# Probabilities and values split into parts and multiplied over 512 queries in three attention stages

## What is computed

```python
# neighbourhood: each query sees a clamped 8 x 16 window of the grid
s = einsum('bhrcd,bhrikd->bhrcik', qg, kg) * d ** -0.5 + bias
s = where(valid[:, None, :], s, NEG)
pr = softmax(s.reshape(B, H, R, GRID_W, kr * GRID_W), axis=-1)
o = einsum('bhrcik,bhrikd->bhrcd', pr, vg)            # then times silu(z)

# dilated: three (window, dilation) bands, each minus slope * |distance|,
# weighted by their softmax denominators (one softmax with multiplicities)
s = q @ k.T * Dh ** -0.5 - slope * abs(pos_q - pos_k)
o = softmax(s + log(multiplicity)) @ v

# latent: 64 + 32 wide queries and keys, 64 wide values, all 1024 keys
s = (qn @ kn.T + qr @ kr.T) * scale
o = softmax(s) @ v
```

## Time and profile before

| | us |
|---|---|
| median of 3 runs (4722.29 to 4726.23) | 4722.94 |
| the profiled execution | 4719.33 |
| its span, first to last instruction | 4717.5 |
| PE busy, mean granted clock 0.944 | 4091.2 (87%) |
| DVE busy | 2223.5 (47%) |
| POOL busy | 1734.4 (37%) |
| ACT busy | 1502.9 (32%) |

### The profile page before, as it was taken

The page is one execution under the profiler, slowest core; times in us unless marked ns, Lnnn a source line. Parts: engine busy times, 40 slices in busy tenths (PEclk is TensorE's granted clock), DMA queues, the critical chain, the costliest instruction groups (busy, mean ns, idle before and its releaser), DMA issues.

```text
span 4717.5 us, 60741 instructions
## 1 busy us (share of the span) xinstructions
PE 4091.2 (87%) x22152; PEld 3489.1 (74%) x22152; DVE 2223.5 (47%) x4269; ACT 1502.9 (32%) x2417; POOL 1734.4 (37%) x1140
## 2 busy tenths in 40 slices
PE   2999665888689798997899999698998995999998
PEld 1888555777578687886688888576887884888887
DVE  2443585532466565553444443465665543233323
ACT  2221233431233674441211221333773432222221
POOL 2433123531354462002444444453660013444442
PEclk8999888999899899998999999799999997999999
DMA  6665332631135422222123221245323221111111
GB/s 156 195 176 154 100 89 64 137 99 49 72 94 139 105 72 53 48 71 82 63 85 107 77 98 32 85 112 147 79 55 68 48 92 40 41 54 50 49 45 50
DMA packets 300704, 404.65 MB, mean 86 GB/s; under 512 B 45908, under 2 KB 224980, under 8 KB 299860
## 3 DMA queue, kind: packets, MB, share of 16 engines
q1 hardware_dynamic: 293496, 375.60, 28.5%
q10 hardware_dynamic: 6912, 25.17, 1.9%
HBM read 316.23 MB, written 93.63 MB: 87 GB/s over the span
## 4 chain that ended last, share of the span: by engine, by line
PE 67%; issue 8%; DVE 7%; POOL 5%; ACT 3%; DMA 3%; DVEq 2%; SPq 2%; POOLq 1%; ACTq 0%
PE ps L849 10%; PE ps L449 6%; PE ps L450 5%; PE ps L451 5%; PE ps L839 5%; PE ps L1788 5%; PE ps L1789 5%; PE ps L1790 5%; PE ps L1804 5%; PE ps L1806 4%; PE ps L1805 4%; POOL rs L738 2%; PE ps L885 1%; PE ps L886 1%; PE ps L1475 1%
## 5 line engine op out<-in xcount | busy, mean ns | idle before, releaser
L404 POOL TENSOR_TENSOR WL<-RAW,WH 128x1024 fp32r<-128x1024 f32 x226 | 556.2, 2473 | 1194.9 <-ACT WH L386 1184.6
L449 PE MATMUL ps<-WH,XTh 128*128 128x512 f32 (+1 forms) x1536 | 611.6, 398 | 47.7 <-POOL XTl L498 25.1
L451 PE MATMUL ps<-WL,XTh 128*128 128x512 f32 (+1 forms) x1536 | 601.0, 391 | 0.0
L450 PE MATMUL ps<-WH,XTl 128*128 128x512 f32 (+1 forms) x1536 | 600.9, 391 | 0.0
L386 ACT ACTIVATE WH<-RAW 128x1024 fp32r<-128x1024 f32 x226 | 234.5, 1063 | 826.1 <-PE ps L1806 347.7
L1824 DVE TENSOR_TENSOR X<-ps,X 128x512 f32<-128x512 f32 x512 | 349.1, 689 | 254.1 <-PE ps L1806 253.1
L1788 PE MATMUL ps<-XTh,WH 128*128 128x512 f32 x1024 | 401.7, 392 | 18.4 <-POOL XTl L498 18.4
L1804 PE MATMUL ps<-WH,Hh 128*128 128x512 f32 x1024 | 401.2, 392 | 4.0 <-DVE X L1824 3.3
L1789 PE MATMUL ps<-XTl,WH 128*128 128x512 f32 x1024 | 400.6, 391 | 0.0
L1790 PE MATMUL ps<-XTh,WL 128*128 128x512 f32 x1024 | 400.4, 391 | 0.0
L1805 PE MATMUL ps<-WH,Hl 128*128 128x512 f32 x1024 | 398.7, 389 | 0.0
(11 more groups left out here) (196 smaller groups left out, 7680.5 us busy)
## 6 DMA issues: line engine op xcount, KB each, us to landing
RAW<-w_all SPq DMA_DIRECT2D x232, 512.0 KB, 3.7
WM<-w_mod ACTq DMA_DIRECT2D x48, 512.0 KB, 4.3
WM<-w_mod SPq DMA_DIRECT2D x48, 512.0 KB, 4.1
QS<-QA_d SPq DMA_DIRECT2D x24, 512.0 KB, 3.8
KHs<-KA_d SPq DMA_DIRECT2D x48, 256.0 KB, 6.1
KLs<-KA_d SPq DMA_DIRECT2D x48, 256.0 KB, 6.8
VS<-VA_d SPq DMA_DIRECT2D x20, 512.0 KB, 7.2
X<-x SPq DMA_DIRECT2D x2, 4096.0 KB, 13.9
```

The costliest lines, as they stand in the source:

```text
L404: e.tensor_tensor(w_low(n), w_raw(n), w_high(n).bitcast(F32), ALU.subtract).then_inc(w_ready, 1)
L449: e.matmul(bank, a, w, start=(kc == 0), stop=False)
L450: e.matmul(bank, b, w, start=False, stop=False)
L451: j = e.matmul(bank, a, l, start=False, stop=(kc == K - 1))
```

## The change

`softmax_pv_pe`, `biased_body`, `out_loop` and the loops of `mla_attention` go; one program for all three stages (`Heads`, `heads_sp`, `heads_pe`, `heads_act`, `heads_dve`, `heads_pool`) takes their place, with one run of 64 units. What is different in it:

- The turned probabilities are split: ACT writes the high part `PTh` in fp32r for both banks (one instruction each), DVE subtracts it from the PSUM bank into the low part `PTl` (one instruction each). The transposes of the next unit into a bank wait for `lo`, the semaphore of that subtraction.
- The values are split once per head: ACT `value_high`, POOL `value_low`, side by side in one tile `VHL` (64 columns high, 64 low).
- Four units make a group G of 512 queries. `values` multiplies `VHL` as weights with `PTh` and with `PTl`, 512 columns wide, into bank 6: 2 x 8 matmuls (2 x 6 in na, where parts of a tile that a query tile doesn't see are zeroed at the start) for a group, in thirds over the next three units. The result has 64 rows of high and 64 of low values; ACT copies it out (`copy_out`, `OT`), and PE turns it back and adds the halves in one step, four matmuls with `twoI` (two unit matrices of 64 above each other) as the moving side, 64 columns (`turn_back`). DVE's `output` handles four tiles at once.
- The maximum is taken negated, so `nmx` falls away.
- In dil ACT computes `slope * distance` for even units only, after exps(u + 1) and not before it; for odd units POOL does it (`TENSOR_SCALAR`).
- In na `NAB` is loaded before values and gate; its wait is for POOL's last bias of head h - 2, not for the output. Queries and keys wait for the scores alone. Values have semaphores of their own.
- The order per unit is PE: scores(u + 1), turn(u), a third of values or turn_back; ACT: exps(u + 1), [distances], [copy_out], high(u), [value_high]; DVE: maxes(u + 1), low(u), [output].

```diff
+            return [sb("PTh" + n, [P, 2, keys, 512], F32R, c), sb("PTl" + n, [P, 2, keys, 512], F32R, c),
+                    sb("VS" + n, [P, 2, T, P], c=c), sb("VHL" + n, [P, 2, T, P], F32R, c), sb("OT" + n, [P, 2, 512], c=c)]
...
+        def heads_pe(who, a):
+            e, s = who.e, a.s
+            half = a.W // 2
+            scores_read = s["exp"] if a.kind == "mla" else s["max"]
+            def scores(u):
+                h, t = divmod(u, T)
+                if t == 0:
+                    e.wait_ge(*a.loaded(h))
+                ge(e, scores_read, a.u0 + u - 1)
...
+                j.then_inc(s["full"], 1)
+            def turn(u):
+                n = len(a.tiles(u % T))
+                e.wait_ge(s["exp"], a.u0 + u + 1)
+                for b in range(2):
+                    ge(e, s["lo"], 2 * (a.u0 + u) - 1 + b)
+                    for k in range(4 * b, min(4 * b + 4, n)):
+                        j = e.transpose(ps[:, 4 + b, (k % 4) * P:(k % 4) * P + P], a.P[:, u % 2, k * P:k * P + P], ident[:])
+                    j.then_inc(s["tr"], 1)
+            def values(G, part):
+                h, g = divmod(G, 2)
+                keys = a.group(g)
+                if part == 0:
+                    e.wait_ge(s["lo"], 8 * (a.g0 + G + 1))
+                    e.wait_ge(s["vlo"], a.h0 + h + 1)
+                    ge(e, s["ot_copied"], a.g0 + G)
+                third = (len(keys) + 2) // 3
+                for n in range(third * part, min(third * part + third, len(keys))):
+                    v = a.VHL[:, h % 2, keys[n], :]
+                    e.matmul(ps[:, 6, :], v, a.PTh[:, G % 2, n, :], start=(n == 0), stop=False)
+                    j = e.matmul(ps[:, 6, :], v, a.PTl[:, G % 2, n, :], start=False, stop=(n == len(keys) - 1))
+                if part == 2:
+                    j.then_inc(s["ot"], 1)
+            def turn_back(G):
+                e.wait_ge(s["ot_copied"], a.g0 + G + 1)
+                ge(e, s["out"], a.g0 + G)
+                for r in range(4):
+                    j = e.matmul(ps[:, 7, 64 * r:64 * r + 64], a.OT[:, G % 2, r * P:r * P + P], twoI[:], start=True, stop=True)
+                j.then_inc(s["back"], 1)
...
+            for u in range(N_UNITS + 4):
+                G, r = divmod(u, 4)
+                if u + 1 < N_UNITS:
+                    scores(u + 1)
+                if u < N_UNITS:
+                    turn(u)
+                if G >= 1 and r < 3:
+                    values(G - 1, r)
+                if G >= 1 and r == 3:
+                    turn_back(G - 1)
...
+        def heads_act(who, a):
+            e, s = who.e, a.s
+            def exps(u):
+                e.wait_ge(s["max"], a.u0 + u + 1)
+                to = a.P[:, u % 2, 0:a.W]
+                if a.kind == "mla":
+                    ge(e, s["tr"], 2 * (a.u0 + u) - 2)
+                    e.activation(to, ps[:, 2 * (u % 2):2 * (u % 2) + 2, :].rearrange("p b c -> p (b c)"), ACT.Exp,
+                                 bias=mx[:, u % 4:u % 4 + 1], accum_out=rl[:, u % 16:u % 16 + 1]).then_inc(s["exp"], 1)
+                else:
+                    e.activation(to, to, ACT.Exp, bias=mx[:, u % 4:u % 4 + 1], scale=-1.0,
+                                 accum_out=rl[:, u % 16:u % 16 + 1]).then_inc(s["exp"], 1)
+            def distances(u):
+                h, t = divmod(u, T)
+                ge(e, s["max"], a.u0 + u - 1)
+                e.activation(BId[:, 0, :], DIST[:, t, :], ACT.Copy, scale=SL[:, h:h + 1]).then_inc(s["dist"], 1)
+            def high(u):
+                G, r = divmod(u, 4)
+                t = u % T
+                n, n0 = len(a.tiles(t)), a.at(t)
+                if r == 0:
+                    ge(e, s["ot"], a.g0 + G - 1)
+                for b in range(2):
+                    k0, k1 = 4 * b, min(4 * b + 4, n)
+                    e.wait_ge(s["tr"], 2 * (a.u0 + u) + 1 + b)
+                    e.activation(a.PTh[:, G % 2, n0 + k0:n0 + k1, r * P:r * P + P],
+                                 ps[:, 4 + b, 0:(k1 - k0) * P].rearrange("p (k q) -> p k q", q=P), ACT.Copy).then_inc(s["hi"], 1)
+            def copy_out(G):
+                e.wait_ge(s["ot"], a.g0 + G + 1)
+                ge(e, s["back"], a.g0 + G - 1)
+                e.activation(a.OT[:, G % 2, :], ps[:, 6, :], ACT.Copy).then_inc(s["ot_copied"], 1)
+            def value_high(h):
+                e.wait_ge(*a.v_loaded(h // 2))
+                ge(e, s["ot"], a.g0 + 2 * h - 2)
+                o0 = 64 * (h % 2)
+                e.activation(a.VHL[:, h % 2, :, 0:64], a.VS[:, h // 2 % 2, :, o0:o0 + 64], ACT.Copy).then_inc(s["vhi"], 1)
+            value_high(0)
+            if a.kind == "dil":
+                distances(0)
+            exps(0)
+            for u in range(N_UNITS + 4):
+                G, r = divmod(u, 4)
+                if u + 1 < N_UNITS:
+                    exps(u + 1)
+                if a.kind == "dil" and u % 2 == 0 and u + 2 < N_UNITS:
+                    distances(u + 2)
+                if G >= 1 and r == 3:
+                    copy_out(G - 1)
+                if u < N_UNITS:
+                    high(u)
+                if u % T == 5 and u + 3 < N_UNITS:
+                    value_high(u // T + 1)
+        def heads_dve(who, a):
+            e, s = who.e, a.s
+            def maxes(u):
+                e.wait_ge(s["full"], a.u0 + u + 1)
+                m = mx[:, u % 4:u % 4 + 1]
+                if a.kind == "mla":
+                    e.tensor_reduce(m, ps[:, 2 * (u % 2):2 * (u % 2) + 2, :].rearrange("p b c -> p (b c)"), AX_X, ALU.max,
+                                    negate=True).then_inc(s["max"], 1)
+                    return
+                e.wait_ge(s["bias"], a.own + u + 1)
+                ge(e, s["tr"], 2 * (a.u0 + u) - 2)
+                B = BIn if a.narrow else BId
+                e.tensor_tensor_reduce(a.P[:, u % 2, 0:a.W].rearrange("p (b c) -> p b c", b=2),
+                                       ps[:, 2 * (u % 2):2 * (u % 2) + 2, 0:a.W // 2],
+                                       B[:, u % 2, 0:a.W].rearrange("p (b c) -> p b c", b=2),
+                                       -1.0, 3e38, ALU.add, ALU.min, m)
+                e.drain().then_inc(s["max"], 1)
+            def low(u):
+                G, r = divmod(u, 4)
+                t = u % T
+                n, n0 = len(a.tiles(t)), a.at(t)
+                for b in range(2):
+                    k0, k1 = 4 * b, min(4 * b + 4, n)
+                    e.wait_ge(s["hi"], 2 * (a.u0 + u) + 1 + b)
+                    at = (slice(None), G % 2, slice(n0 + k0, n0 + k1), slice(r * P, r * P + P))
+                    e.tensor_tensor(a.PTl[at], ps[:, 4 + b, 0:(k1 - k0) * P].rearrange("p (k q) -> p k q", q=P),
+                                    a.PTh[at].bitcast(F32), ALU.subtract).then_inc(s["lo"], 1)
+            def output(G):
+                h, g = divmod(G, 2)
+                e.wait_ge(s["back"], a.g0 + G + 1)
+                c = 4 * G % 16
+                e.reciprocal(li[:], rl[:, c:c + 4])
+                e.drain()
+                got = ps[:, 7, 0:256].rearrange("p (t c) -> p t c", t=4)
+                to = Y[:, 4 * g:4 * g + 4, a.ycol + 64 * h:a.ycol + 64 * h + 64]
+                each = bc3(li[:], 4, 64)
+                if a.narrow:
+                    o0 = 64 * (h % 2)
+                    tmp = TMPn[:].rearrange("p (t c) -> p t c", t=4)
+                    e.tensor_tensor(tmp, got, each, ALU.mult)
+                    e.drain()
+                    e.tensor_tensor(to, tmp, ZSn[:, h // 2 % 2, 4 * g:4 * g + 4, o0:o0 + 64], ALU.mult).then_inc(s["out"], 1)
+                else:
+                    e.tensor_tensor(to, got, each, ALU.mult).then_inc(s["out"], 1)
+            maxes(0)
+            for u in range(N_UNITS + 5):
+                G, r = divmod(u, 4)
+                if u + 1 < N_UNITS:
+                    maxes(u + 1)
+                if u < N_UNITS:
+                    low(u)
+                if G >= 2 and r == 0:
+                    output(G - 2)
...
+        def heads_pool(who, a):
+            e, s = who.e, a.s
+            def value_low(h):
+                e.wait_ge(s["vhi"], a.h0 + h + 1)
+                o0 = 64 * (h % 2)
+                e.tensor_tensor(a.VHL[:, h % 2, :, 64:128], a.VS[:, h // 2 % 2, :, o0:o0 + 64],
+                                a.VHL[:, h % 2, :, 0:64].bitcast(F32), ALU.subtract).then_inc(s["vlo"], 1)
+            def far(u):
+                h, t = divmod(u, T)
+                ge(e, s["max"], a.u0 + u - 1)
+                if a.kind == "na":
+                    if t == 0:
+                        e.wait_ge(*a.loaded(h))
+                        nab = NAB[:, h % 2, :].rearrange("p (a b) -> p a b", b=GRID_W)
+                        e.tensor_tensor(nab, nab, rows3(CMK[:], NA_E, GRID_W), ALU.add)
+                        e.drain()
+                    e0 = (NA_START[t] - 2 * t + 8) * GRID_W
```

(15 more changed lines are left out.)

382 lines of the change are left out of this document (136 added, 246 removed).

## The result

The changed kernel takes 5222.69 us (median of 4 runs, 5220.88 to 5227.75), the kernel before 4723.24 beside it (4722.29 to 4726.23): a ratio of 1.106, 95% interval 1.104 to 1.108. It is slower by 499 us, where 332 were forecast; 5223 lies above the upper end of the range, 5160. The direction and the kind of cause hold, the size doesn't.

A forecast was written before the change was run, and what follows sets the result against it. PE was taken to bound mla and dil, a chain over a load na. 4719.3 + 45 + 2 x 110 + 2 x 33 = 5050; with 3.6 for the median and under 2 for the rest, 5055 us, range 4900 to 5160.

The forecast's parts named there:

- The closed loop DVE, ACT, DVE: All three stages: maximum, exponential and splits run in a row without overlap, setting the unit time, 4.62 us in mla.
- the even step of dil: In dil, ACT's late distances and POOL's sum delay the maximum after an even unit: 6.3 us between maxima.
- `NAB` off the chain: In na, the load at a head's start no longer delays units: under 20 us needed, eight units give 30.
- `PTlm` waiting for ACT's `PThm`: Sign in mla: DVE's low-part subtraction waits for ACT's high part, with DVE's reductions 4.6 us apart.
- the rival that PE stays the bound: All three stages: handovers overlap and the busiest engine sets the time, 4530 us in total; chance 0.06.
- dil at 5.5 a unit with the product hidden: In dil, a pair takes 11.0 us, with POOL's odd-unit product taken as hidden; +110 us, twice.
- na at 3.76 a unit: In na, a unit takes 3.76 us against 3.24 before; stage 252 against 207.3 us, +45.
- ends and starts of the stages: Outside the repeated units: ends of 10 us in mla and dil, 8.7 in na; starts 1 later in mla, 0.6 in dil.
- What is late next: Passage claiming the order of DVE's and ACT's queues sets the unit time wherever over PE's 3.6, 3.1 or 2.2 us.
- 0.25 a unit: PE's work for turning back: 4 float32 matmuls in 8 records, at most 1.0 us for four units.
- the once-a-group pieces: copy_out on ACT, 0.12 us a unit, and output on DVE, 0.15 (0.28 in na), each a group's duration over four.
- PE's clock falls: Rival: PE at its lower clock level needs 6.2 us a unit in dil, 4.4 in na; +130, 5185 us; chance 0.08.

The follow-up runs named there:

- the combination: Against the changed kernel: turn_back a group later, ACT's split and copy_out before the exponential, ACT computing all distances three units ahead, low value parts later; 4578.07 us.

## Why the prediction was right in its direction and wrong in its size

**Right.** The closed loop DVE, ACT, DVE behind the queues' order: 4.18 us in mla for 4.35, the even step of dil 6.2 for 6.3, `NAB` off the chain, `PTlm` waiting for ACT's `PThm`. Only the kernels with ACT's split first cut this loop; in all others the plain unit of mla stays at 4.18. Against the rival that PE stays the bound: it named its own condition, "as soon as ACT's exponential doesn't hold back high(u)", and once that and the other waits are gone, the combination gives 4578 for its 4530. The rule that the prediction took from the Trainium skill (Perfetto Trace Analysis, Identifying the Most-Contended Engine), to optimise the engine with the highest occupancy first, names PE here, and the combination shows that there was something to be had from it; by itself the rule doesn't tell whether a change gets it, as the 5223 show.

**Wrong, term by term**, against the 5055 (the intervals of the runs, times 63 units and the number of stages):

| step of the prediction | us |
|---|---|
| `turn_back` and the wait for `copy_out`, not in the loop at all: intervals of after less those with it a group later, (0.355 + 2 x 0.348 + 2 x 0.576) x 63 | +139 |
| dil at 5.5 a unit with the product hidden: 5.76 without the long unit | +33 |
| na at 3.76 a unit, without POOL's three instructions in a row at a head's start: 4.104 less 3.764 | +21 |
| the loop itself shorter than forecast: mla 4.41 for 4.62, na 3.75 less those 0.34 for 3.76 (in mla the way from ACT's split to the next maximum takes 1.82, not 1.97) | -48 |
| ends and starts of the stages: growth outside the intervals, some 35 where the forecast had some 10; not followed up | +25 |
| sum | +170 |

The measured miss is 168. That it isn't 216 is luck: the handovers of the loop were put too long, and that hides a part of the rest. The step that failed is under "What is late next": it followed DVE's and ACT's queues for what each waits for, but of PE only the work was counted, "0.25 a unit" for turning back, and the once-a-group pieces were taken as durations to be divided by four. `copy_out` was given its own 0.50 us; who waits for it (PE's `turn_back`), and what stands behind that waiter (the scores), was not asked. The rows of the queues that stand ahead of the prediction are of ACT, DVE and POOL; PE's were not looked at in the same way.

**The clock.** The sum had it at nothing. The rival "PE's clock falls" took it as a loss of rate over whole stages, 130 us, and in that form it didn't come. Where it costs, in mla above all, it comes as a short wait of PE and the matmuls behind it at 1.2 GHz, inside the long unit, so it is part of the +139, and the run with the useless matmuls gives its share: some 76 us. In dil the granted clock stays at 0.82 without the long unit too, while the steps of 5.33 and 6.20 are those of POOL's path: there PE is slow and nobody waits for it. The 0.97 of `diff_attention` was no guide to the stages after, which have 0.79, 0.80 and 0.86.

**The product.** 1.2 was half of the sum's 2.38, and 2.38 was held to be the upper end. It took 2.84, outside both ends, and by the row of dil above that cost is in the +33. The Trainium skill (GPSIMD Engine Reference, Engine selection) has one-input operations at roughly line rate; the trace doesn't agree, here one input with a scale per partition takes longer than two inputs:

```profile
L1533 POOL TENSOR_SCALAR BId<-DIST,SL 128x1024 f32<-128x1024 f32 x64 | 182.0, 2843 | 0.0
...
L1535 POOL TENSOR_TENSOR BId<-BId,TB 128x1024 f32<-128x1024 f32 x128 | 302.1, 2360 | 274.1 <-ACT BId L1408 264.7
```

(Groups of the kernel after by line: count | busy us, mean ns of one | idle before.)

**Slips in the working** that change nothing: 1.4 + 1.04 + 1.95 is 4.4 us, not 4.3 (the interval of mla before was 4.12), and in an even step of dil DVE would be free at 5.6, not 5.5.

**The range.** Its upper end had parts of the clock's and of the product's cost as single additions and no room for a wait that was not listed.
